# Long request's keys: two pairs of expansion banks and a new order of the phases on PE, ACT and DVE

## The reference, cut to what matters

```python
def _mla(cq, ckv, kr, q_norm_w, w_uq, kv_norm_w, w_ukv, attn_norm_w):
    ...
    kv = (_rmsnorm(ckv, kv_norm_w) @ w_ukv).reshape(b, s, N_HEADS_ATTN, QK_NOPE_DIM + V_HEAD_DIM)
    k_nope, v = jnp.split(kv, [QK_NOPE_DIM], axis=-1)
    k_rope = _rope(kr, cos, sin)
    ...
```

## Time and profile before

| | us |
|---|---|
| median of 3 executions | 2921.43 |
| lowest, highest | 2920.6, 2926.34 |
| the profiled execution, its own time | 2920.38 |
| its span, first to last instruction | 2918.6 |
| PE busy in it | 2756.9 (94%) |
| DVE busy, ACT busy | 2164.3 (74%), 1522.0 (52%) |
| mean granted clock of PE | 0.981 |

### The profile page before, as it was taken

The page is one execution under the profiler, slowest core; times in us unless marked ns, Lnnn a source line. Parts: engine busy times, 40 slices in busy tenths (PEclk is TensorE's granted clock), DMA queues, the critical chain, the costliest instruction groups (busy, mean ns, idle before and its releaser), DMA issues.

```text
span 2918.6 us, 50438 instructions
## 1 busy us (share of the span) xinstructions
PE 2756.9 (94%) x17762; PEld 2395.3 (82%) x17762; DVE 2164.3 (74%) x4178; ACT 1522.0 (52%) x2880; POOL 217.2 (7%) x188
## 2 busy tenths in 40 slices
PE   5999788899999959999999999999999999999997
PEld 4999555566667849999999999999999999999995
DVE  3564786676765587878878878878778778788786
ACT  4443445445444335555555555555556555555554
POOL 0000022121210000000000000000000000000001
PEclk8999899999999979999999999999999999999999
DMA  7121310212216528768767778677677777677674
GB/s 262 68 64 60 123 40 31 78 72 104 85 53 242 185 86 274 244 219 259 236 231 252 229 238 261 219 239 253 222 256 237 225 248 247 224 244 252 216 240 173
DMA packets 359354, 546.66 MB, mean 187 GB/s; under 512 B 14608, under 2 KB 287760, under 8 KB 359248
## 3 DMA queue, kind: packets, MB, share of 16 engines
q1 hardware_dynamic: 352304, 520.88, 52.5%
q0 software_dynamic: 6944, 24.38, 4.0%
HBM read 493.51 MB, written 51.71 MB: 187 GB/s over the span
## 4 chain that ended last, share of the span: by engine, by line
PE 55%; DVE 4%; issue 2%; ACT 1%; DMA 0%; DVEq 0%; ACTq 0%; POOLq 0%
PE banks L2896 24%; PE banks L2909 16%; PE banks L2897 11%; PE banks L2869 4%; DVE weights_low L2662 1%; PE banks L2836 1%; DVE h_or_keys_or_sums L2753 1%; DVE weighted L2708 1%; DVE hidden L2763 0%; ACT h_or_keys_or_sums L2610 0%; DVE hidden_parts L2765 0%; DVE hidden_parts L2768 0%; DVE keys_or_w_out L2802 0%; DMA rows<-normed,chosen 0%; DVE slab_down L2809 0%
## 5 line engine op out<-in xcount | busy, mean ns | idle before, releaser
L2896 PE MATMUL banks<-rowsT_parts,weights_high 128*128 128x384 f32 x4096 | 1213.8, 359 | 11.8 <-DVE hidden_parts L2768 7.8
L2897 PE MATMUL banks<-rowsT_parts,weights_low 128*128 128x192 f32 x4096 | 1026.8, 251 | 0.0
L2897 PEld LDWEIGHTS banks<-rowsT_parts,weights_low 128*128 128x128 f32 x4096 | 781.8, 191 | 22.5
L2896 PEld LDWEIGHTS banks<-rowsT_parts,weights_high 128*128 128x128 f32 x4096 | 770.6, 188 | 22.3 <-DVE hidden_parts L2768 10.5
L2662 DVE TENSOR_TENSOR weights_low<-keys_or_w_out,weights_high 128x1024 fp32r<-128x1024 f32 x512 | 603.3, 1217 | 1.4 <-ACT weights_high L2584 1.4
L2584 ACT ACTIVATE weights_high<-keys_or_w_out 128x1024 fp32r<-128x1024 f32 x512 | 523.7, 1049 | 22.0 <-PEq L2044 22.0
L2753 DVE TENSOR_TENSOR h_or_keys_or_sums<-banks,h_or_keys_or_sums 128x192 f32<-128x192 f32 x512 | 181.4, 354 | 317.3 <-ACT h_or_keys_or_sums L2610 317.2
L2909 PE MATMUL banks<-weights_high,hidden_parts 128*128 128x512 f32 x1536 | 403.7, 391 | 0.0
L2610 ACT ACTIVATE h_or_keys_or_sums<-banks 128x192 f32<-128x192 f32 x512 | 165.5, 323 | 451.0 <-PE banks L2869 333.2
L2909 PEld LDWEIGHTS banks<-weights_high,hidden_parts 128*128 128x128 f32 x1536 | 283.5, 188 | 56.0
L2662 DVE TENSOR_TENSOR weights_low<-slab_down,weights_high 128x1024 fp32r<-128x1024 f32 x256 | 311.4, 1216 | 0.0
(11 more groups left out here) (338 smaller groups left out, 3661.5 us busy)
## 6 DMA issues: line engine op xcount, KB each, us to landing
keys_or_w_out<-w_gate SPq DMA_DIRECT2D x128, 1024.0 KB, 5.6
keys_or_w_out<-w_up SPq DMA_DIRECT2D x128, 1024.0 KB, 7.1
slab_down<-w_down SPq DMA_DIRECT2D x128, 1024.0 KB, 4.9
arena_attend<-w_ada SPq DMA_DIRECT2D x8, 2048.0 KB, 7.8
arena_attend<-ssd_tiles SPq DMA_DIRECT2D x12, 992.0 KB, 9.2
arena_inputs<-w_ada SPq DMA_DIRECT2D x4, 2048.0 KB, 11.5
ssd_tiles<-arena_inputs SPq DMA_DIRECT2D x24, 256.0 KB, 2.1
mixed<-arena_attend SPq DMA_DIRECT2D x12, 512.0 KB, 2.9
```

The costliest lines, as they stand in the source:

```text
L2896: nc.tensor.matmul(out[:, 0:2 * CT], w_hi[:, u, block], x[:, k, :], start=k == 0, stop=False)
L2897: mm = nc.tensor.matmul(out[:, 0:CT], w_lo[:, u, block], x[:, k, 0:CT], start=False, stop=k == KD - 1)
```

## The change

For request 1 (r = 1) alone:

- `expand` writes tiles of even j to banks 1 and 2 as before, and tiles of odd j to banks 6 and 7 (`kv_banks`); `take_kv` reads there.
- The lists of the three engines have another order. In turn t, PE does `turn_c` of t + 2, `expand` of t + 1, `turn_k` of t; ACT does `turned_c` of t + 2, `take_kv` of t + 1, `take_kT` of t, `stats` of t + 3; DVE does `take_kv` of t + 1, `take_kT` of t, `norm` of t + 3.
- Waits are added: `turn_c` for the copy of the former turned latent (`cT_done`), `turn_k` for the two copies of the former turned keys (`kT_act`, `kT_dve`), DVE's `take_kv` for its own former copies (`kn_done`).

Request 0 keeps its code.

```diff
--- before.py
+++ after.py
@@ -1157,6 +1157,10 @@
     turned, cT_done, kv_mm, rot_order = sem("ckv_turned"), sem("ckvT_done"), sem("kv_mm"), sem("k_rot_order")
     kn_done, v_done, k_turned, kT_act, kT_dve = (sem(n) for n in ("kn_done", "v_done", "k_turned", "kT_act", "kT_dve"))
 
+    def kv_banks(j):
+
+        return core.ps[6:8] if r and j else core.ps[1:3]
+
     def latent(g, lo, hi):
 
         return nat[:, bass.ds(g, 1), lo:hi].rearrange("p o c -> p (o c)")
@@ -1187,7 +1191,7 @@
         def take_kv(g, i, j):
             act.wait_ge(kv_mm, g + 1)
 
-            kv = core.ps[1].rearrange("p (h e) -> p h e", h=4)
+            kv = kv_banks(j)[0].rearrange("p (h e) -> p h e", h=4)
             nc.scalar.activation(kn[j][:, 0:4, 0:DN], kv[:, :, 0:DN], ACT.Copy)
             nc.scalar.activation(v[:, bass.ds(i * 512, 256)].rearrange("p (h e) -> p h e", h=4), kv[:, :, DN:],
                                  ACT.Copy).then_inc(v_done, 1)
@@ -1196,7 +1200,10 @@
             act.wait_ge(k_turned, g + 1)
             nc.scalar.activation(kT[0:DQK, 0:4, bass.ds(i * P, P)],
                                  core.ps[3][0:DQK, :].rearrange("p (h t) -> p h t", h=4), ACT.Copy).then_inc(kT_act, 1)
-        request_pipeline(act, r, [(0, take_kT), (1, take_kv), (2, turned_c), (3, stats)], beside)
+        if r:
+            request_pipeline(act, r, [(2, turned_c), (1, take_kv), (0, take_kT), (3, stats)], beside)
+        else:
+            request_pipeline(act, r, [(0, take_kT), (1, take_kv), (2, turned_c), (3, stats)], beside)
 
     def on_dve(dve, beside):
         dve.wait_ge(sem(f"kv_in{r}"), 16)
@@ -1208,7 +1215,8 @@
 
         def take_kv(g, i, j):
             order = Order(dve, rot_order, g)
-
+            if r:
+                dve.wait_ge(kn_done, g)
             kr = latent(g, KVL, KVL + DR)
             ropes = core.rope[:, bass.ds(i, 1)].rearrange("p o s f -> p (o s f)")
             spread = [t.unsqueeze(1).broadcast_to([P, NH, 16]) for t in rot]
@@ -1219,7 +1227,7 @@
             nc.vector.tensor_tensor(kn[j][:, :, DN:DN + 16], spread[0], spread[1], ALU.subtract)
             nc.vector.tensor_tensor(kn[j][:, :, DN + 16:], spread[2], spread[3], ALU.add)
             dve.wait_ge(kv_mm, g + 1)
-            kv = core.ps[2].rearrange("p (h e) -> p h e", h=4)
+            kv = kv_banks(j)[1].rearrange("p (h e) -> p h e", h=4)
             nc.vector.tensor_copy(kn[j][:, 4:8, 0:DN], kv[:, :, 0:DN])
             nc.vector.tensor_copy(v[:, bass.ds(i * 512 + 256, 256)].rearrange("p (h e) -> p h e", h=4),
                                   kv[:, :, DN:]).then_inc(kn_done, 1)
@@ -1228,30 +1236,41 @@
             dve.wait_ge(k_turned, g + 1)
             nc.vector.tensor_copy(kT[0:DQK, 4:8, bass.ds(i * P, P)],
                                   core.ps[4][0:DQK, :].rearrange("p (h t) -> p h t", h=4)).then_inc(kT_dve, 1)
-        request_pipeline(dve, r, [(0, take_kT), (1, take_kv), (3, norm)], beside)
+        if r:
+            request_pipeline(dve, r, [(1, take_kv), (0, take_kT), (3, norm)], beside)
+        else:
+            request_pipeline(dve, r, [(0, take_kT), (1, take_kv), (3, norm)], beside)
 
     def on_pe(pe, beside):
         pe.wait_ge(sem("w_ukv_in"), 16)
 
         def turn_c(g, i, j):
             pe.wait_ge(cn_done, g + 1)
+            if r:
+                pe.wait_ge(cT_done, g)
             nc.tensor.transpose(core.ps[0][:, 0:P], cn[j][:, QL:], core.ident).then_inc(turned, 1)
 
         def expand(g, i, j):
             pe.wait_ge(cT_done, g + 1)
             for half in range(2):
-                mm = nc.tensor.matmul(core.ps[1 + half], cT[j][:, 2, :], wukv[:, 512 * half:512 * half + 512],
+                mm = nc.tensor.matmul(kv_banks(j)[half], cT[j][:, 2, :], wukv[:, 512 * half:512 * half + 512],
                                       start=True, stop=True)
             mm.then_inc(kv_mm, 1)
 
         def turn_k(g, i, j):
             pe.wait_ge(kn_done, g + 1)
             pe.wait_ge(v_done, g + 1)
+            if r:
+                pe.wait_ge(kT_act, g)
+                pe.wait_ge(kT_dve, g)
             for h in range(NH):
                 mm = nc.tensor.transpose(core.ps[3 + h // 4][0:DQK, h % 4 * P:(h % 4 + 1) * P], kn[j][:, h, :],
                                          core.ident)
             mm.then_inc(k_turned, 1)
-        request_pipeline(pe, r, [(0, turn_k), (1, expand), (2, turn_c)], beside)
+        if r:
+            request_pipeline(pe, r, [(2, turn_c), (1, expand), (0, turn_k)], beside)
+        else:
+            request_pipeline(pe, r, [(0, turn_k), (1, expand), (2, turn_c)], beside)
     return load, on_act, on_dve, on_pe
 
 
```

## The result

The changed kernel takes 2935.43 us (median of 5 runs, 2934.98 to 2940.18) against 2921.43 us of the kernel before (5 runs, 2920.24 to 2927.24). The ratio is 1.0047, with a 95% interval of 1.0036 to 1.0058: slower by some 14 us.

The account below looks back on a forecast made before the run. PE bounds the experts' part, untouched; the keys stage waits for DVE's copies. Removing 6.4 us of rest but adding a 5.12 us ring with a half-cold clock gave +17.5 on 2920.38, a median of 2938.9 us, range 2927 to 2946.

Parts of the forecast that it names:

- PE's rest ahead of the keys' turning: Long request's keys stage: PE's wait for DVE's copy from the expansion's bank, 6.4 us in 8 tiles, would go.
- The ring: Keys stage: each latent's turning waits through PE, ACT's copy, statistics and norm; 5.12 us at full clock, PE resting about 2.2.
- the sum: Step times of the keys stage added up, with the full clock as early as now: first scores at 540.9, +7.6 us.
- The opening: Start of the keys stage: latent's turnings at 497.67, 499.84 and 506.0; first expansion 1.49 us later.
- Case B: Keys stage with half of the work at either clock level: +17.5 us, 2938.9 us as a median; chance 0.62.
- A: Rival: keys stage with the ring and the full clock: +7.6 us, 2929.0 us as a median; chance 0.20.
- C: Rival: keys stage all at 1.2 GHz, ring 7.96 us: +27 to +31 us, 2949 to 2953; chance 0.07.
- the tail: Keys stage from the eighth and last latent's turning to the first scores: 532.5 to 540.9 at the full clock.
- The new wait at the end: Eighth keys' turning waits for DVE's copy of the seventh to free the bank: 1.0 us later, at 538.9.
- Rival E: The stage's loss is absorbed later, for instance by loads that start with it: 2921 us; chance 0.06.
- Rival D: No ring in the keys stage, statistics don't hold PE up: -4.3 us, 2917 us; chance 0.05.

Follow-up runs that it names:

- e1: Kernel before with only the second pair of banks added, old order and waits kept: 2923.3 us, ratio 0.9999.
- e8: Changed kernel with two idle products on PE behind the keys' turning of turns 0 to 5, into bank 0, after a wait for the latent's copy: 2931.8 us, ratio 1.0035.
- e3: Changed kernel with ACT's statistics right behind the latent's copy and DVE's norm first in its turn: 2917.3 us, ratio 0.9977 to the kernel before.
- e5: Changed kernel with the new order on PE alone, ACT and DVE in the order of the kernel before: 2947.8 us, ratio 1.0088.
- e7: e3 with DVE's rotation put ahead of the norm and its copies behind it: 2917.8 us, ratio 0.9981 to the kernel before.
- e2: Changed kernel with one pair of banks, each expansion waiting for the former tile's copies: 2934.0 us, ratio 1.0036 to the kernel before.
- e6: e3 with one pair of banks, each expansion waiting for the former tile's copies: 2921.2 us, ratio 1.0000 to the kernel before.
- e4: Changed kernel with two idle products on PE behind the keys' turning of turns 0 to 5, into bank 5: 2933.9 us, ratio 1.0029.

## Why the prediction was right, point by point

- **The change doing what it says.** PE's rest ahead of the keys' turning went, as said; the banks by themselves gave nothing (e1, ratio 0.9999).
- **The ring.** It was there, with its five steps: 0.50 + 1.10 + 0.42 by the rows after for the copy, the statistics and the norm, where the sum had 0.50 + 1.15 + 0.43. Its length at the full clock was 5.07 (e8) and 5.07 (514.08 to 519.15 in the changed kernel), for 5.12. That it is the place of the statistics that makes it was shown both ways: opened in e3, the loss is gone; lengthened in e5, it grows.
- **The opening.** Second turning 2.08 after the first against 2.17 in the sum, third at 7.94 against 8.3.
- **Case B, the clock.** The swing was forecast as half of the work at either level. That half was the middle between A and C and not worked out from a row; that it came near is in part luck. The four rings from 514.08 to 539.03 took 24.95 us, 6.24 each, for B's 6.54 (the measured ring stands at 0.4 of the way from A's 5.12 to C's 7.96); the fourth turning came 14.5 after the first, where B's mean had 15.3. Between A and C the measured stage (+12.1) lies nearer to A (+7.6) than the middle does (+17.5).
- **The mis-sized term is the tail.** From the last latent's turning to the first scores B had half of A's 8.4 and C's 14.9, 11.7 us. Measured: 8.27 (539.03 to 547.30). After the last norm nothing rests, and the clock was up when that run began and stayed up. That is 3.4 of the 5.4 us by which the stage was forecast too long; the cold share of the rings and of the opening is the rest.
- **The total.** +14.0 us as medians for +17.5 forecast is nearer than the stage, +12.1. The 1.9 us by which the total exceeds the stage need not be the change's: the executions of before beside the changed kernel had a median of 2921.4 us, and two later sets of 21 had 2923.0 and 2923.1, against which the loss would be 12.3 to 12.5.
- **Slips of the text that change no forecast.** The stage from 497.24 to 533.26 is 36.0 us and not some 37. Case C, 2949 to 2953, lies wholly outside the range that ends at 2946, and not half of it.
- **The new wait at the end** was there, 0.9 us ahead of the last keys' turning, for DVE's copy L1237, for the 1.0 of the sum; at mid-stage the added waits cost nothing.
- **Downstream.** The shift went through whole: from the first scores to the end 2385.3 us before and 2385.9 after (2385.3 to 2387.5 over all ten traces). Rival E falls. Rival D, no ring, is what e3 and e7 are, and the gain of 4.3 that the sum gave it was even passed (6.9 and 8.1 in the stage).
- **The rule of the Trainium skill cited for B** (page "TensorE: Matmul & The Clock Gate", section "A second HAM failure mode: psum-queue depth-cycling") agrees with the trace in its effect: the clock swings between its two levels three tiles running. The page names the going round through banks together with the short rests; here it is the rests that count, since e2 with one pair of banks swings too, and e1 with two pairs in the old order does not once its clock is up.

## What to carry to other kernels

In a software pipeline written as phases on in-order engines, look for the step that stands last in one engine's turn and feeds the first step of another engine's next turn: such a pair closes a ring through everything between, and here it cost 2.1 us a tile where the wait that was removed had cost 0.7. A second pair of banks is worth what the trace shows PE waiting for a bank, which was nothing before, and 0.5 us a tile only once the order let PE run ahead. When a rest is put into PE's stream, count the clock too: here it was 1.2 us of a ring's 6.2, and 5.0 of the 12.1 us that the stage lost.

## What the runs showed of the hardware that I had not expected

The clock's swing locked in with the ring: in three tiles running the expansion was granted 1.2 GHz and the keys' turning 2.4 GHz, after PE had worked 1.15 to 1.30 of 3.30 us ahead of each fall. Idle products in the rest made the whole stage 3.3 us shorter, and its last four rings 5.0 us.

Code that no kernel here changes did not take the same time in each profiled execution. From the first latent's turning of the prompt to that of the long request it was 155.6 us before (342.09 to 497.67) and in e2, 156.8 in the changed kernel, e6 and e8, 157.2 in e1 and 159.6 in e3, e4, e5 and e7, with the same PE instructions and a lower mean clock in places. e4 and e8 differ by a bank and one wait, and still by 2.8 us here. One such place in the kernel before and then in e7, about the same work but not to the last row:

```profile
460.00:480.00 20.00, 17.64 (x111) 12.16 (x109) 15.09 (x36) 12.46 (x37) 3.75 (x2) 1.00 0.24 84
```

```profile
463.00:483.00 20.00, 18.19 (x91) 11.72 (x90) 12.94 (x30) 12.46 (x37) 1.44 (x2) 0.83 0.23 84
```

A difference of 4 us ahead of the stage in one profiled execution is therefore not put down to the change. Since each kernel has one trace, it isn't shown how much of it one kernel has from execution to execution. The stage and the medians have to be read side by side.
